# Pool matrices in the gate-sum buffer, their products a block earlier and on the band only, five loads issued by GpSimd

## What is computed

```python
def multiscale_pool_mixer(u, pool_w, pool_scale):      # u: (1, 256, 512), four groups of 128 channels
    ...
    for g, w in enumerate((2, 4, 8, 16)):
        mean = (sum of the last w tokens of group g) / min(t + 1, w)
        z = mean - u[group g]
        outs.append(z @ pool_w[g])                     # 128 x 128
    return concatenate(outs) * pool_scale

proj = x @ w_in                                        # 2048 -> 7176 columns
(q, k, v, g_att, fg, c_b, c_c, c_h, g_conv, p_u, g_pool) = split(proj)
y_att  = forgetting_attention(q, k, v, fg, b_f) * silu(g_att)
y_conv = short_conv_mixer(c_b, c_c, c_h, conv_w) * silu(g_conv)
y_pool = multiscale_pool_mixer(p_u, pool_w, pool_scale) * silu(g_pool)
y = concatenate([y_att, y_conv, y_pool]) @ w_out       # 2048 x 2048
out = layer_norm_2(2 ** 0.25 * x + y, ln_g, ln_b)
```

## Time and profile before

| | |
|---|---|
| median of 3 runs | 2666.75 us |
| lowest and highest run | 2663.47 and 2667.16 us |
| profiled execution | 2661.63 us |
| its span, first to last instruction | 2659.8 us |
| granted clock of TensorE, mean | 0.998 of full |
| busy: TensorE, VectorE, ScalarE, GpSimd | 99%, 60%, 48%, 9% |

### The profile page before, as it was taken

The page is one execution under the profiler, slowest core; times in us unless marked ns, Lnnn a source line. Parts: engine busy times, 40 slices in busy tenths (PEclk is TensorE's granted clock), DMA queues, the critical chain, the costliest instruction groups (busy, mean ns, idle before and its releaser), DMA issues.

```text
span 2659.8 us, 35264 instructions
## 1 busy us (share of the span) xinstructions
PE 2622.5 (99%) x12267; PEld 2177.3 (82%) x12267; DVE 1591.3 (60%) x2577; ACT 1277.4 (48%) x2401; POOL 249.4 (9%) x386
## 2 busy tenths in 40 slices
PE   9999999999999999999999999999999999999998
PEld 7778877888888888888788888888888888888876
DVE  6876756665656565555555556556565555565766
ACT  6553345545454444445455545444544444435443
POOL 1000000031313120000000031313130000000000
PEclk9999999999999999999999999999999999999999
DMA  7553233656566666566555656565656665555564
GB/s 223 176 160 92 75 101 111 197 183 204 183 196 189 189 205 192 191 191 216 178 175 187 194 187 198 181 205 182 204 185 202 191 190 154 174 175 172 178 237 158
DMA packets 251154, 477.48 MB, mean 180 GB/s; under 512 B 19080, under 2 KB 22912, under 8 KB 250400
## 3 DMA queue, kind: packets, MB, share of 16 engines
q1 hardware_dynamic: 245808, 467.92, 56.3%
q10 hardware_dynamic: 4656, 7.15, 0.7%
q0 software_dynamic: 576, 0.90, 0.2%
HBM read 473.82 MB, written 2.10 MB: 179 GB/s over the span
## 4 chain that ended last, share of the span: by engine, by line
PE 92%; DVE 5%; ACT 1%; issue 1%; DMA 0%; ACTq 0%; SPq 0%; POOL 0%; DVEq 0%
PE ps L1041 28%; PE ps L1043 28%; PE ps L1042 28%; DVE gs L1258 1%; PE ps L822 1%; DVE w_lo L1541 1%; PE ps L1106 1%; PE ps L1092 1%; ACT w_hi L720 0%; DVE gs L1256 0%; PE ps L1184 0%; PE ps L1168 0%; PE ps L1096 0%; PE ps L1027 0%; PE ps L1025 0%
## 5 line engine op out<-in xcount | busy, mean ns | idle before, releaser
L1541 DVE TENSOR_TENSOR w_lo<-raw,w_hi 128x512 fp32r<-128x512 f32 (+1 forms) x1776 | 1186.1, 706 | 733.0 <-ACT w_hi L720 730.2
L720 ACT CAST w_hi<-raw 128x512 fp32r<-128x512 f32 (+1 forms) x1776 | 1033.6, 623 | 728.3 <-PE ps L1043 517.6
L1041 PE MATMUL ps<-w_hi,xh 128*128 128x512 f32 (+1 forms) x2464 | 969.5, 393 | 7.7 <-DVE w_lo L1541 6.9
L1043 PE MATMUL ps<-w_hi,xl 128*128 128x512 f32 (+1 forms) x2464 | 956.8, 388 | 0.0
L1042 PE MATMUL ps<-w_lo,xh 128*128 128x512 f32 (+1 forms) x2464 | 955.9, 388 | 0.0
L1041 PEld LDWEIGHTS ps<-w_hi,xh 128*128 128x128 f32 x2464 | 462.9, 188 | 106.4 <-DVE w_lo L1541 15.5
L1043 PEld LDWEIGHTS ps<-w_hi,xl 128*128 128x128 f32 x2464 | 462.6, 188 | 96.2
L1042 PEld LDWEIGHTS ps<-w_lo,xh 128*128 128x128 f32 x2464 | 463.1, 188 | 90.5
L1041 PE MATMUL ps<-w_hi,fh 128*128 128x512 f32 x1056 | 415.2, 393 | 5.5 <-DVE w_lo L1541 5.5
L1043 PE MATMUL ps<-w_hi,fl 128*128 128x512 f32 x1056 | 412.0, 390 | 0.0
L1042 PE MATMUL ps<-w_lo,fh 128*128 128x512 f32 x1056 | 411.7, 390 | 0.0
(11 more groups left out here) (295 smaller groups left out, 1095.5 us busy)
## 6 DMA issues: line engine op xcount, KB each, us to landing
raw<-in_ffn_w_gate SPq DMA_DIRECT2D x176, 512.0 KB, 4.5
raw<-in_ffn_w_up SPq DMA_DIRECT2D x176, 512.0 KB, 4.5
raw<-in_ffn_w_down SPq DMA_DIRECT2D x176, 512.0 KB, 4.4
raw<-in_w_in SPq DMA_DIRECT2D x112, 512.0 KB, 4.0
raw<-in_even_w_in SPq DMA_DIRECT2D x80, 512.0 KB, 3.6
raw<-in_odd_w_in SPq DMA_DIRECT2D x64, 512.0 KB, 4.5
raw<-in_even_w_out SPq DMA_DIRECT2D x32, 512.0 KB, 3.8
raw<-in_odd_w_out SPq DMA_DIRECT2D x32, 512.0 KB, 4.8
```

The costliest lines, as they stand in the source:

```text
L720: act.copy(w_tile(w_hi, w2_hi, blk, k), raw[:, slot, kk, 0:blk.width]).then_inc(hi_ready, 1)
L1041: pe.matmul(acc(blk, t), hi_x[:, blk.kt0 + k, tok], hi_w, start=(k == 0), stop=False)
L1043: ins = pe.matmul(acc(blk, t), lo_x[:, blk.kt0 + k, tok], hi_w, start=False, stop=(k == blk.nk - 1))
L1541: TT(w_tile(w_lo, w2_lo, blk, k), raw[:, slot, kk, 0:w], w_tile(w_hi, w2_hi, blk, k).bitcast(F32), ALU.subtract).then_inc(lo_ready, 1)
```

## The change

- `poolm` now lies in `extra`, where the gate sums were; `poolw` and `zT` lie in `sga`. Only `gf_row` stays at its old address.
- The five loads go from ScalarE's step to GpSimd, behind its last norm root: `poolm` after `h_nm` 8, `poolw` after `h_ya` 16, and the three rows when TensorE is through with `gp`.
- The band products move from k = 2 of `final` j = 0 to k = 6 of `gp`. Per group, the first half of the tokens is multiplied for 144 output tokens, the second half for its own 128; the columns left out hold zeros.
- The copies to `zT` move to VectorE's k = 8 of `gp`, the products with `poolw` to TensorE's k = 11 of `gp`.
- ScalarE's wait for `pw_mm` ahead of the last block goes.

```diff
-        poolm, poolw, zT, gf_row = overlay(("poolm", [P, NT, 4, SEQ]), ("poolw", [P, 4, P]),
-                                           ("zT", [P, 4, SEQ]), ("gf_row", [P, D]))
+        _, gf_row = overlay(("pad_g", [P, 3584]), ("gf_row", [P, D]))
+        poolm = extra[:, :, :].rearrange("p (t w) q -> p t w q", t=NT)
+        poolw = sga[:, 0, 0:BLK].rearrange("p (g c) -> p g c", g=4)
+        zT = sga[:, 1, :].rearrange("p (g q) -> p g q", g=4)
...
@@ ScalarE, during @@
                 if blk.kind == "final" and blk.j == 0:
-                    if k == 0:
-                        act.wait_ge(mm_done, blk.k0)
-                        act.dma_start(poolm[:, :, :, :], a["pool_consts"].rearrange("(t p) w q -> p t w q", p=P)
-                                      ).then_inc(pool_loaded, 16)
-                        act.dma_start(poolw[:, :, :], a["pool_w_2"][0].rearrange("g c d -> c g d")).then_inc(pool_loaded, 16)
-                        act.dma_start(gf_row[:, :], a["final_norm"].unsqueeze(0).to_broadcast([P, D])).then_inc(gf_loaded, 16)
-                        act.wait_ge(h_pv, 8)
-                        act.dma_start(ln2_g_row[:, :], a["ln_g_2"].to_broadcast([P, D])).then_inc(ln2_loaded, 16)
-                        act.dma_start(ln2_b_row[:, :], a["ln_b_2"].to_broadcast([P, D])).then_inc(ln2_loaded, 16)
...
@@ TensorE, during @@
-                if blk.kind == "final" and blk.j == 0:
-                    if k == 2:
+                if blk.kind == "gp":
+                    if k == 6:
                         pe.wait_ge(pool_loaded, 32)
+                        pe.wait_ge(h_lo, 8)
                         pe.wait_ge(evac_dve, by["pu"][0].n_dve)
                         for g in range(4):
-                            for t in range(NT):
-                                ins = pe.matmul(halves(6 + g // 2)[:, g % 2, :], pun[:, t, P * g:P * (g + 1)],
-                                                poolm[:, t, g, :], start=(t == 0), stop=(t == 1))
+                            z = halves(6 + g // 2)[:, g % 2, :]
+                            pe.matmul(z[:, 0:P + 16], pun[:, 0, P * g:P * (g + 1)], poolm[:, 0, g, 0:P + 16],
+                                      start=True, stop=True)
+                            ins = pe.matmul(z[:, P:2 * P], pun[:, 1, P * g:P * (g + 1)], poolm[:, 1, g, P:2 * P],
+                                            start=False, stop=True, skip_group_check=True)
                         ins.then_inc(z_mm, 1)
-                    if k == 5:
+                    if k == 11:
                         pe.wait_ge(z_copied, 2)
...
@@ VectorE, during @@
+                if blk.kind == "gp" and k == 8:
+                    dve.wait_ge(z_mm, 1)
+                    dve.wait_ge(h_ya, 16)
+                    for c in range(2):
+                        dve.tensor_copy(zT[:, 2 * c:2 * c + 2, :], halves(6 + c)).then_inc(z_copied, 1)
                 if blk.kind == "final" and blk.j == 0:
-                    if k == 5:
-                        dve.wait_ge(z_mm, 1)
-                        for c in range(2):
-                            dve.tensor_copy(zT[:, 2 * c:2 * c + 2, :], halves(6 + c)).then_inc(z_copied, 1)
...
@@ GpSimd @@
             inverse_root(rstd[:, 4, :], ms, 2, ms_ready, 5, rstd_ready)
+            gp.wait_ge(h_nm, 8)
+            gp.dma_start(poolm, a["pool_consts"].rearrange("(t p) w q -> p t w q", p=P)).then_inc(pool_loaded, 16)
+            gp.wait_ge(h_ya, 16)
+            gp.dma_start(poolw, a["pool_w_2"][0].rearrange("g c d -> c g d")).then_inc(pool_loaded, 16)
+            gp.wait_ge(mm_done, by["final"][0].k0)
+            gp.dma_start(gf_row[:, :], a["final_norm"].unsqueeze(0).to_broadcast([P, D])).then_inc(gf_loaded, 16)
+            gp.dma_start(ln2_g_row[:, :], a["ln_g_2"].to_broadcast([P, D])).then_inc(ln2_loaded, 16)
+            gp.dma_start(ln2_b_row[:, :], a["ln_b_2"].to_broadcast([P, D])).then_inc(ln2_loaded, 16)
```

More of the change, by code:

```diff
@@ L714, in stream @@
                             act.wait_ge(x_out, 4)
-                            act.wait_ge(pw_mm, 1)
                         if k >= RING:
```

## The result

| | before | after |
|---|---|---|
| median of 20 runs each, us | 2664.20 | 2658.71 |
| lowest to highest | 2661.01 to 2667.87 | 2655.63 to 2660.31 |
| ratio, 95% interval | | 0.9978, 0.9972 to 0.9984 |
| span of the profiled execution | 2659.8 | 2655.2 |

The change makes the kernel faster by 5.5 us (5.9 by the ratio); the interval allows 4 to 7.5. The forecast was 2662 us (2662.15 unrounded) with a gain of 4.6. Of the 3.4 us between 2662.15 and 2658.71, 2.55 lie in the kernel before, whose median is 2664.20 over 20 runs and was 2666.75 over the three shown; 0.9 is gain beyond the sum. The span of the profiled execution is 4.6 us less, which is the sum predicted.

The account below looks back on a forecast made before the run. TensorE, busy 99% of the span, was taken to bound the kernel. Gains of 3.0 (hole) and 1.6 (band products), 4.6 us off the 2666.75 us median, gave 2662 us; range for 8 in 10: 2657 to 2666.5.

Parts of the forecast that it names:

- The term of the band products: Pool gate's block: narrower band products, 144 and 128 columns for two of 256; gain 1.6 us, bounds 0.85 and 1.7.
- The term of the hole: First output block: TensorE's hole after the first tile closes; gain 3.0 us, bounds 0 and 3.0.
- step (a): First output block: ScalarE's wait and five load issues go, so TensorE's hole closes; gain 3.0 us.
- Rival E: Weight stream gains elsewhere, as by a shorter rush of loads, or median shown is high; 2657 to 2660 us, chance 0.08.
- the likeliest case: Whole kernel: hole closed, band products cut; 2662 us, gain just under the 0.2% bound, chance 0.65.
- this chance: Whole kernel: faster by over 0.2%, chance 0.42; within 0.2%, chance 0.53.
- (c): Pool gate's block: new waits of TensorE at k = 6 and VectorE at k = 8; cost 0.
- (d): First output block: VectorE's slack shrinks to 0.9 us at k = 16, no stall; cost 0, bounds 0 and 2 us.
- Rival B: First output block: normalisations or late weight load stop TensorE at k 12 to 16; saving 1.6 to 4 us, chance 0.16.
- Step (e): Five loads on GpSimd's queue, three of them at the first output block's start: nothing late; cost 0.
- D's price: First output block: gf_row lands late from GpSimd's queue; slower, 2673 us for a 30 us landing, chance 0.07.
- Rival C: First output block: ScalarE still waits for same matmul three steps later, hole stays; saving 1.6, 2665 us, chance 0.04.

Follow-up runs that it names:

- b1: The kernel before, unchanged, profiled once more; 1.7 us of clock missing behind the hole.
- b2: The kernel before, unchanged, profiled once more; 3.4 us of clock missing, TensorE lost 2.9 us by the starts of its matmuls.
- c0: The changed kernel measured again, against the kernel before on the same chip; 2657.25 us, ratio 0.9974.
- b3: The kernel before, unchanged, profiled once more; no clock missing behind the hole.
- c1: The kernel before with only the band products narrowed to 144 and 128 columns, still in their old place; 2662.30 us, ratio 0.9993.
- c2: The changed kernel with full-width band products of 256 columns in the new place; 2660.67 us, ratio 0.9981.
- d1: The changed kernel with ScalarE's wait for the block before kept in the first output block, no loads issued there; 2663.01 us, ratio 0.9993.
- d2: The changed kernel with the three norm rows issued by ScalarE in the first output block, behind its old wait; 2661.42 us, ratio 0.9993.
- d3: The changed kernel with two extra additions on VectorE at k = 12 of the first output block; 2659.62 us, ratio 0.9988.
- f1: The changed kernel with ScalarE's old wait kept and GpSimd's norm rows issued three tiles later; one execution, span 2657.4 us.
- c3: The kernel before with its five loads moved to GpSimd and ScalarE's wait gone, buffers and pool products as before; 2663.18 us, ratio 0.9995.
- d4: The changed kernel with the three norm rows issued only after nine tiles of the first output block; 2664.90 us, ratio 1.0004.

## Why the prediction was right, and where it was short

**The sum.** The term of the band products was 1.6 us; measured 3.45 - 1.87 = 1.6. A record of 144 columns took 0.125 us against my 0.122. The term of the hole was 3.0 us; the hole is gone, and the profiled executions differ by the sum, 4.6 us. That the spans agree to the tenth is in part luck: both have one stretch at half clock near 440 us and none elsewhere, while b1, b2 and c0 have more. The two places themselves do not depend on it: T0 came within 0.1 us of its forecast, and behind T0 TensorE does not stand.

**The term that was mis-sized** is this second one, step (a): I priced the hole with the one execution shown, in which nothing followed it. Of the five profiled executions with the hole of 3 us (before, b1, b2, b3, c1), the half clock behind it cost 0, 1.7, 2.9, 0 and 1.7 us, 1.3 on average. Of the seven whose longest stand in the output block was under 2 us (after, c0, c2, d1, d2, d3, f1) none has any there. With them the hole costs 4.3 us and the change should bring 5.9; measured 5.5 and 7.1 us. That the half clock is there is shown; that it makes up the whole difference between 4.6 and the medians is an estimate from five executions. The mean granted clock that is on record for every execution points the same way, weakly: 0.9973 and 0.9974 in the two sets of 31 executions of the kernel before, 0.9976 in the 29 of the changed one, and 0.0002 to 0.0003 of 2660 us is 0.5 to 0.8 us; but c1 and c3, which have a hole, show 0.9977 and 0.9978. The page "TensorE: Matmul & The Clock Gate" of the Trainium skill, in "Part 1: The HAM clock gate (the "warmup" mystery)", has the rule that an idle TensorE falls back to 1.2 GHz; these rows agree where the clock fell, and before and b3, with the same hole at full clock, show that it need not fall. I could have seen the scatter in front: the profiled execution stood 5.1 us below the median of its three runs. Each of the 14 profiled executions also stands 2.0 us near 290 us and 2.1 us near 440 us (the second in the profile of before is shown below), and half clock follows in 7 of them at the first place and in 12 at the second. This is a part of the scatter of runs that I had named and not explained.

```profile
PE ps L1041 <- DVE w_lo L1541: 2.1, 1, 2.1
```

**Rival E** (more than the sum) is thus nearest to the medians, though the mechanism I named for it, a shorter rush, was not it. The chance of it, 0.08, was too small. The gain, 0.22% by the ratio, lies just beyond the 0.2% under which I had put the likeliest case; the interval (0.16% to 0.28%) holds both sides, so that this chance, 0.42 against 0.53, is not decided by the result.

**Steps (c) and (d)** held to 0.2 us, and d3 shows the slack of 0.9 us. But the reason that I gave for a cost of 0 in (d), a median landing of 5.0 us, was not what happened: the load for k = 12 fell into the rush and took 8.9 us, and only the bound of 9.9 was right. In f1 such a load, for k = 14 and issued later, took 13.5 us and cost 1.6 us at k = 14 to 16. Rival B is therefore real, and the change stays clear of it by 1 us.

**Step (e).** The rule of the Trainium skill ("SBUF — State Buffer", section "SBUF: two separate sides") on descriptors that GpSimd cannot write beside VectorE's two-port copies changed nothing here: three loads of 1 MB landed in 4.9, 7.1 and 10.2 us. No run here had a two-port copy at that moment, so the rule itself stays untested. D's price was too kind: a late load also lands later, in d4. And its example is added up wrongly: by its own rule a landing of 30 us, 11 beyond the 19 that cancel the gain, gives 2677.7 us and not 2673. A slip of the same kind, without weight: ScalarE stood 8.8 us from the end of its cast to its first issue; the 9.5 is from the start of that cast.

**Rival C** is ruled out by the profile after: ScalarE still waits 4.43 us for the same matmul, three steps later, and TensorE has no hole. With the wait at its old step, d1, TensorE stands 0.4 us at once and 3.2 us more behind it; f1 shows that the 2.6 of these at k = 8 and 9 come from a weight load that the wait delays into the rush. What causes the 0.6 us at k = 15 and 16 was not tested.

**Open:** the spans of c0 and after, the same kernel, differ by 2.7 us. All of it arises ahead of the places that the edit touches (T0 is 2559.40 and 2556.66 us). One stretch at half clock near 290 us is 1.7 of it, and the rest stands by 70 us, when the same product starts at 70.70 and 69.58 us; there, near the start, c0's first products wait 0.5 us more for the load of x. The new place with all five loads still on ScalarE was not run; d2, which leaves three of them there, still has a hole of 1.75 us.

## What to carry over

When an engine that feeds the bottleneck waits in the step where it also issues loads, price three things: the lead that the wait drains, the time of each issue, and the loads further back that are released late and then land in the rush. Data with a fixed use late in a kernel belongs in a buffer that is free a block earlier: moving the queue alone moved the stall (3.0 to 2.6 us), moving the place with it removed it. And before trusting one profiled execution, compare it with the median: what it lacks may be a cost that only some executions pay.

## What the runs showed of the hardware

A TensorE that had stood 2.6 to 5.5 us ran on, in four of seven executions, at a granted 1.2 GHz for a while, in which a matmul of 512 columns took 0.43 us instead of 0.227; 1.7 us were lost each time, once 2.9. Stands of 0.3 to 1.9 us in the same block were followed by none. Elsewhere in the kernel shorter stands were: half clock followed the one of 2.0 us near 290 us in 7 of 14 executions, and the one of 2.1 us near 440 us, with 0.5 and 1.0 us just ahead of it, in 12 of 14. The granted clock fell within the hole in b2, 0.9 us before the next matmul, and 1.2 us after the first matmul behind it in b1 and c1.

Three loads of 1 MB, issued within 1.6 us by GpSimd, landed after 4.9, 7.1 and 10.2 us, and made 512 KB loads of SP's queue, 4.7 us in the median, take 8.9 (after), 11.0 (d1) and 13.5 us (f1).
